# Choosing the 16 best key pairs per token from 112 rank pairs in place of 256, on VectorE alone

## The reference, cut to what matters

```python
def peer_token_block(xb, w_pq, peer_keys, peer_u, peer_v):
    qh = (xb @ w_pq).reshape(t, PEER_HEADS, 2, PEER_QDIM // 2)       # 8 heads, two halves
    s = jnp.einsum('thpc,hpkc->thpk', qh, peer_keys)                  # 128 scores for each half
    s_top, i_top = lax.top_k(s, PEER_TOPK)                            # the 16 best of each half
    cand = s_top[:, :, 0, :, None] + s_top[:, :, 1, None, :]          # 16 x 16 pairs
    cand_idx = i_top[:, :, 0, :, None] * PEER_NKEYS + i_top[:, :, 1, None, :]
    best, pos = lax.top_k(cand.reshape(t, PEER_HEADS, 256), PEER_TOPK)
    idx = jnp.take_along_axis(cand_idx.reshape(...), pos, axis=-1)    # 16 experts per head
    g = jax.nn.softmax(best, axis=-1)
    ...

def encoder_layer(...):
    ffn = channel_mixer(h, w_pq, peer_keys, peer_u, peer_v)
    ple = jax.nn.sigmoid(h @ w_pg) * (p @ w_pe)
    return layer_norm(DEEPNORM_ALPHA * h + ffn + ple, ln2_g, ln2_b)
```

## Time and profile before

| | |
|---|---|
| runs, us | 4625.53, 4610.86, 4606.46 |
| median | 4610.86 |
| span of the profiled execution | 4614.7 |
| busy, share of the span | PE 82%, DVE 73%, PEld 44%, ACT 28%, POOL 21% |
| `best_pairs` (first DMA to the last `g_low`) | about 1530.6 to 1972 us from the start |

### The profile page before, as it was taken

How to read it: one execution, slowest core, us unless ns; L and a number is a source line. 1 busy time by engine, 2 the same in 40 slices (tenths; PEclk the granted TensorE clock), 3 DMA queues, 4 the chain that set the end, 5 groups by cost and what they waited for, 6 DMA issues and landing times. The chain is left out here.

```text
span 4614.7 us, 58881 instructions
## 1 busy us (share of the span) xinstructions
PE 3770.5 (82%) x19550; PEld 2045.0 (44%) x19550; DVE 3353.4 (73%) x5560; ACT 1271.7 (28%) x2566; POOL 989.7 (21%) x1048
## 2 busy tenths in 40 slices
PE   7946667997899233389989999999999999999994
PEld 3525543553455111156644444444444445444442
DVE  1043341222589799976659999999999999999998
ACT  2132132222233111133333333333333323333321
POOL 0000000000000000000024434443444444444444
PEclk9966588998999567655579999999999999999997
DMA  2200012101110100034478898898888888888885
GB/s 87 82 3 0 0 79 101 42 14 64 43 41 26 58 0 0 0 108 134 142 252 327 327 335 316 330 341 320 322 338 330 325 334 331 332 335 330 326 321 191
DMA packets 234207, 852.35 MB, mean 185 GB/s; under 512 B 15952, under 2 KB 115088, under 8 KB 162704
## 3 DMA queue, kind: packets, MB, share of 16 engines
q0 software_dynamic: 73728, 536.90, 30.9%
q1 hardware_dynamic: 160400, 314.42, 19.6%
HBM read 790.45 MB, written 60.82 MB: 184 GB/s over the span
## 5 line engine op out<-in xcount | busy, mean ns | idle before, releaser
L69 PE MATMUL x_ps_v<-x_v_hi,x_w_hi 128*128 128x512 f16 x1536 | 605.8, 394 | 134.5 <-DVE x_w_lo L1648 73.9
L1547 POOL DMA_INDIRECT x_rows<-in_peer_uv,x_index x512 | 589.9, 1152 | 408.1 <-POOL x_index L1544 393.1
L1618 DVE SCALAR_TENSOR_TENSOR acc<-x_rows,x_share,acc 128x1024 f32<-128x1024 f32 x512 | 655.3, 1280 | 0.0
L1702 PE MATMUL x_ps_a<-h_hi,x_u_hi 128*128 128x256 f16 (+1 forms) x2048 | 620.2, 327 | 16.7 <-ACT x_u_hi L1560 16.7
L1703 PE MATMUL x_ps_a<-h_lo,x_u_hi 128*128 128x256 f16 (+1 forms) x2048 | 620.1, 327 | 0.0
L1544 POOL COPY x_index<-expert 128x1 uint32 (+1 forms) x512 | 337.8, 660 | 1260.9 <-DVE acc L1618 868.3
L70 PE MATMUL x_ps_v<-x_v_lo,x_w_hi 128*128 128x512 f16 x1536 | 603.6, 393 | 0.0
L71 PE MATMUL x_ps_v<-x_v_hi,x_w_lo 128*128 128x512 f16 x1536 | 602.2, 392 | 0.0
L1571 ACT ACTIVATE x_dots<-x_dots 128x1 f32<-128x1 f32 x512 | 103.9, 203 | 1333.7 <-DVE x_dots L1636 1333.7
L1208 POOL TENSOR_TENSOR b_hits_iota<-b_hits_iota,top_i 128x2048 f16<-128x2048 f16 x10 | 38.4, 3842 | 1917.8 <-DVE b_hits_iota L1274 1917.8
L1636 DVE CUSTOM_DVE_ANT_0 x_rows<-h_lo,x_rows 128x1024 f32<-128x1024 f32 x256 | 312.5, 1221 | 121.1 <-DMA x_rows<-in_peer_uv,x_index 120.4
(11 more groups left out here) (279 smaller groups left out, 6747.9 us busy)
## 6 DMA issues: line engine op xcount, KB each, us to landing
x_u_st<-in_peer_u_t SPq DMA_DIRECT2D x128, 512.0 KB
x_v_st<-in_peer_v SPq DMA_DIRECT2D x128, 512.0 KB
gate_scratch<-g_out SPq DMA_DIRECT2D x24, 2048.0 KB, 8.7
x_gate<-gate_scratch SPq DMA_DIRECT2D x32, 1024.0 KB
x_gate<-gate_scratch SPq DMA_DIRECT2D x32, 512.0 KB, 4.2
m_w_st<-in_w_merge SPq DMA_DIRECT2D x8, 1536.0 KB, 6.4
k_w_st<-in_w_route SPq DMA_DIRECT2D x16, 576.0 KB, 3.7
x_rows<-in_peer_uv,x_index POOLq DMA_INDIRECT x512
```

The costliest lines, as they stand in the source:

```text
L69: pe.matmul(out, lhs_hi, rhs_hi, start=first, stop=False)
L1547: pool.indirect_dma_start(rows[:, m % RING], None, uv_all, bass.IndirectOffsetOnAxis(ap=index[:, m % RING:m % RING + 1], axis=0)).then_inc ...
L1618: dve.scalar_tensor_tensor(R.acc[:, DT + tile], rows[:, r, D:2 * D], share[:, s:s + 1], R.acc[:, DT + tile], ALU.mult, ALU.add).then_inc(v ...
L1702: pe.matmul(out, u_hi[:, e, ko], R.h_hi[:, ko, t], start=ko == 0, stop=False)
```

## The change

Only `best_pairs` is changed.

- Of two descending lists of 16, only 112 rank pairs are added up as candidates: the first 4 ranks of the first half with all 16 of the second, and the other 12 ranks with the first 4 of the second. Each pair left out has at least 24 pairs that are not below it. A place among the 112 is turned into two ranks by four `scalar_tensor_tensor` steps (`place`, `rank`), where a shift and a mask did it before.
- The one-hot keeps its size, 256 x 16, but the rank is now the inner index. Each rank number is written twice side by side (`place` has a last axis of two). Both halves are multiplied by the key numbers on DVE, and the 16 products are added by halving: 8 + 8, 4 + 4, 2 + 2 and 1 + 1, each one `tensor_tensor`; the last writes both halves' key numbers to `gij`. POOL and the two reductions are gone from the stage.
- `w_st` and `cand` have their own memory. In the first tile the ten weight splits stand between the five searches, two after each. DVE waits for `steps` ahead of its first tile.
- The denominator's sum stands ahead of the addition to `R.acc` (L1304 before L1306).

The diff, cut to its core (lines of context without a sign):

```diff
+WIDE = 4
+NCAND = WIDE * TOPK + (TOPK - WIDE) * 4
+CANDS = ((0, 0, WIDE, TOPK), (WIDE * TOPK, WIDE, TOPK - WIDE, 4))
...
-        cand = sb("b_cand", [P, PH, TOPK, TOPK], f32)
+        cand = sb("b_cand", [P, PH, NCAND], f32)
...
-        place = pos[:].rearrange("p h k -> p (h k)").bitcast(f16)
...
-        pair = sb("b_hits_iota", [P, 2, TOPK, 2 * P], f16)
-        hits, iota = pair[:, 0], pair[:, 1]
+        rank = sb("b_rank", [P, 2, P], f32)
+        place = sb("b_place", [P, 2, P, 2], f16)
...
+        work = sb("b_hits", [P, KP * NT], f32)
+        hits = work[:, 0:P * TOPK].bitcast(f16).rearrange("p (n a) -> p n a", a=TOPK)
+        iota = sb("b_iota", [P, TOPK], f16)
...
-        w_st = cand[:].rearrange("p h a b -> p (h a b)").rearrange("p (s d) -> p s d", d=D)
-        p_st = pair[:].rearrange("p s a n -> p (s a n)").bitcast(f32)[:, 0:KP * NT].rearrange("p (k t) -> p k t", k=KP)
+        w_st = sb("b_w_st", [P, 2, D], f32)
+        p_st = work[:].rearrange("p (k t) -> p k t", k=KP)
...
-        LINKS = 14
+        LINKS = 19
...
-        def pick(eng, half, t):
-            names = R.top_i[:, half::2, t].rearrange("p h (a b) -> p h a b", b=1).to_broadcast([P, PH, TOPK, TOPK])
-            picked = hits[:, :, half * P:(half + 1) * P].rearrange("p a (h k) -> p h a k", h=PH)
-            return eng.tensor_tensor(picked, picked, names, ALU.mult)
-        @block.gpsimd
-        def _(pool):
-            def tile(t, s, peeled, _):
-                wait_apart(pool, hits_ok, t + 1)
-                pick(pool, 1, t).then_inc(picked_ok, 1)
-            tiles(pool, tile)
         @block.vector
         def _(dve):
-            for k in range(KW):
+            dve.wait_ge(consts, 32)
+            dve.tensor_copy(iota[:], steps[:]).then_inc(iota_ok, 1)
+            dve.wait_ge(iota_ok, 1)
+            def split_w(k):
                 dve.wait_ge(w_hi_ok, k + 1)
                 dve.scalar_tensor_tensor(w_lo[:, k], w_st[:, k % 2], WSCALE, w_hi[:, k], ALU.mult,
                                          ALU.subtract).then_inc(w_lo_ok, 1)
                 if k == 1:
                     dve.wait_ge(p_hi_ok, 1)
                     dve.tensor_tensor(p_lo[:], p_st, p_hi[:], ALU.subtract).then_inc(p_lo_ok, 1)
-            dve.wait_ge(w_lo_ok, KW)
-            dve.wait_ge(p_lo_ok, 1)
-            dve.wait_ge(consts, 32)
-            dve.tensor_copy(iota, steps[:].rearrange("p (a n) -> p a n", n=1).to_broadcast([P, TOPK, 2 * P])
-                            ).then_inc(iota_ok, 1)
-            dve.wait_ge(iota_ok, 1)
             def tile(t, s, peeled, fetched):
                 count = [0]
+                at_start = isinstance(t, int) and t == 0
                 def link(ins):
                     count[0] += 1
                     ins.then_inc(dve_in, 1)
                     wait_apart(dve, dve_in, LINKS * t + count[0])
-                if isinstance(t, int) and t == 0:
-                    pass
-                else:
+                def splits(ks):
+                    if at_start:
+                        for k in ks:
+                            split_w(k)
...
-                first = R.top_v[:, 0::2, t].rearrange("p h (a b) -> p h a b", b=1).to_broadcast([P, PH, TOPK, TOPK])
-                second = R.top_v[:, 1::2, t].rearrange("p h (a b) -> p h a b", a=1).to_broadcast([P, PH, TOPK, TOPK])
-                link(dve.tensor_tensor(cand[:], first, second, ALU.add))
-                rows = [cand[:, h].rearrange("p a b -> p (a b)") for h in range(PH)]
+                first, second = R.top_v[:, 0::2, t], R.top_v[:, 1::2, t]
+                for at, a0, n_a, n_b in CANDS:
+                    a = first[:, :, a0:a0 + n_a].rearrange("p h (a b) -> p h a b", b=1).to_broadcast([P, PH, n_a, n_b])
+                    b = second[:, :, 0:n_b].rearrange("p h (a b) -> p h a b", a=1).to_broadcast([P, PH, n_a, n_b])
+                    out = cand[:, :, at:at + n_a * n_b].rearrange("p h (a b) -> p h a b", b=n_b)
+                    last = dve.tensor_tensor(out, a, b, ALU.add)
+                link(last)
+                rows = [cand[:, h] for h in range(PH)]
                 for h in range(PH):
                     last = dve.max(best[:, h, 0:8], rows[h])
                 link(last)
+                splits((0, 1))
                 for h in range(PH):
                     last = dve.max_index(pos[:, h, 0:8], best[:, h, 0:8], rows[h])
                 link(last)
+                splits((2, 3))
                 for h in range(PH):
                     last = dve.match_replace(rows[h], best[:, h, 0:8], rows[h], LOWEST)
                 link(last)
+                splits((4, 5))
                 for h in range(PH):
                     last = dve.max(best[:, h, 8:16], rows[h])
                 link(last)
+                splits((6, 7))
                 for h in range(PH):
                     last = dve.max_index(pos[:, h, 8:16], best[:, h, 8:16], rows[h])
                 link(last)
+                splits((8, 9))
+                if at_start:
+                    dve.wait_ge(p_lo_ok, 1)
                 dve.tensor_tensor(ex[:], best[:], best[:, :, 0:1].to_broadcast([P, PH, TOPK]),
                                   ALU.subtract).then_inc(dif_ok, 1)
                 flat = pos[:].rearrange("p h k -> p (h k)")
+                twice = lambda ap: ap.rearrange("p (n a) -> p n a", a=1).to_broadcast([P, P, 2])
                 dve.tensor_scalar(part[:, 0], flat, 4, None, ALU.logical_shift_right)
-                link(dve.tensor_scalar(part[:, 1], flat, TOPK - 1, None, ALU.bitwise_and))
-                link(dve.tensor_copy(place, part[:].rearrange("p h n -> p (h n)")))
-                chosen = place.rearrange("p (a n) -> p a n", a=1).to_broadcast([P, TOPK, 2 * P])
-                dve.tensor_tensor(hits, iota, chosen, ALU.is_equal).then_inc(hits_ok, 1)
-                wait_apart(dve, hits_ok, t + 1)
-                if not (isinstance(t, int) and t == 0):
+                link(dve.tensor_scalar(part[:, 1], flat, 2, None, ALU.logical_shift_right))
+                link(dve.scalar_tensor_tensor(place[:, 0], twice(part[:, 1]), float(WIDE - WIDE * 4), twice(part[:, 0]),
+                                              ALU.add, ALU.max))
+                dve.scalar_tensor_tensor(rank[:, 0], place[:, 0, :, 0], -float(TOPK), flat, ALU.mult, ALU.add)
+                link(dve.scalar_tensor_tensor(rank[:, 1], place[:, 0, :, 0], -4.0, flat, ALU.mult, ALU.add))
+                link(dve.scalar_tensor_tensor(place[:, 1], twice(rank[:, 1]), -float(WIDE * TOPK - WIDE * 4),
+                                              twice(rank[:, 0]), ALU.add, ALU.max))
+                steps2 = iota[:].rearrange("p (m a b) -> p m a b", m=1, b=2).to_broadcast([P, 2 * P, TOPK // 2, 2])
+                chosen = place[:].rearrange("p s n (a b) -> p (s n) a b", a=1).to_broadcast([P, 2 * P, TOPK // 2, 2])
+                link(dve.tensor_tensor(hits.rearrange("p n (a b) -> p n a b", b=2), steps2, chosen, ALU.is_equal))
+                for half in range(2):
+                    names = R.top_i[:, half::2, t].rearrange("p h (k a) -> p h k a", k=1).to_broadcast([P, PH, TOPK, TOPK])
+                    picked = hits[:, half * P:(half + 1) * P].rearrange("p (h k) a -> p h k a", h=PH)
+                    last = dve.tensor_tensor(picked, picked, names, ALU.mult)
+                link(last)
+                for n in (8, 4, 2):
+                    link(dve.tensor_tensor(hits[:, :, 0:n], hits[:, :, 0:n], hits[:, :, n:2 * n], ALU.add))
+                if not at_start:
                     wait_apart(dve, t_mm, t)
-                link(pick(dve, 0, t))
-                link(dve.tensor_reduce(gij[:, 1], hits[:, :, 0:P].rearrange("p a n -> p n a"), AX.X, ALU.add))
+                link(dve.tensor_tensor(gij[:, 1:3].rearrange("p s n -> p (s n)"), hits[:, :, 0], hits[:, :, 1], ALU.add))
                 wait_apart(dve, sig, t + 1)
                 dve.scalar_tensor_tensor(s_g[:], ps_p[:], 1 / WSCALE, s_g[:], ALU.mult, ALU.mult).then_inc(prod, 1)
+                wait_apart(dve, exp_ok, t + 1)
+                link(dve.tensor_reduce(den[:, :, 0:1], ex[:], AX.X, ALU.add))
                 wait_apart(dve, prod, t + 1)
...
                 dve.tensor_tensor(R.acc[:, t], R.acc[:, t], s_g[:], ALU.add).then_inc(added, 1)
-                wait_apart(dve, exp_ok, t + 1)
-                link(dve.tensor_reduce(den[:, :, 0:1], ex[:], AX.X, ALU.add))
                 link(dve.reciprocal(den[:, :, 1:2], den[:, :, 0:1]))
-                wait_apart(dve, picked_ok, t + 1)
-                link(dve.tensor_reduce(gij[:, 2], hits[:, :, P:2 * P].rearrange("p a n -> p n a"), AX.X, ALU.add))
                 link(dve.tensor_tensor(gij[:, 0].rearrange("p (h k) -> p h k", h=PH), ex[:],
```

More of the change, by code:

```diff
@@ L1121, in best_pairs @@
         sem = lambda n: R.stack.enter_context(nc.semaphore(n))
-        NC = TOPK * TOPK
         KP = PLE // P
@@ L1149, in best_pairs @@
```

(2 more changed lines are left out.)

## The result

The changed kernel took 4494.06 us (median of 4 runs, 4484.2 to 4498.24), the kernel before on the same chip 4612.43 (4 runs): a ratio of 0.9728, interval 0.9713 to 0.9744. The forecast was 4478 with a range from 4462 to 4512. The profiled execution took 4493.93 us, 1.8 more than its span.

What follows compares the result with a forecast made beforehand. DVE was taken to set the pace of best_pairs from the first tile on. Savings of 10.9 us there and 122.1 in nine tiles took the span from 4614.7 to 4481.7; less 3.8 to the median gave 4478, range 4462 to 4512.

Steps and rivals of the forecast that it cites:

- Adding pairs and searches: Start of each tile on DVE: fewer columns save 1.13 us in the addition and 6.0 us in the searches.
- Rival 4: Searches do not get shorter, only their fixed part counting: +54, 4532 us; chance 0.03, shared with a gain partly lost elsewhere.
- Rival 1: One-hot, perhaps products and first halvings, run at 1.04 ns a column: +22 (4500) or +55 (4533 us); chance 0.11.
- Halvings: Four additions after the products on DVE: 3.56 us a tile together, the last two 0.58 each without links.
- Rival 3: Short hops in the one-hot's operations make the kernel slower, from 1.87 ns an element on: +110, 4720 us; chance 0.02.
- Links: Gaps between linked DVE steps in a tile: 0.11 us each.
- Cover: Later tiles: the sigmoid ends 4.7 us before DVE reaches its step, so neither PE nor ACT is late.
- rival 2: PE becomes the bound, staying at its lower clock for all 60 matmuls: +55, 4533 us; chance 0.07.
- First tile: Splits end at 1570.6, PE starts 4 us later, DVE waits 7.5 us, and the weights come 10.9 us earlier.
- Later stages only start earlier: Stages behind best_pairs: they only start earlier, since dense_gates reads what is complete before it begins.
- From span to median: Last step of the sum: the median of the runs lies 3.8 us below the profile's span.
- the bad end of the halvings: Halvings with every element at the reduction's price: 7.0 us without links, counted as 4.3 us worse a tile.

Runs made afterwards that it cites:

- e7: The changed kernel with PE waiting for each weight block by itself in the first tile, not for all ten: 4481.93 us, ratio 0.9698.
- e1: The kernel before with only the 112 pairs changed; its one-hot, POOL and order of splits kept: 4557.19 us, ratio 0.9857.
- e4: The changed kernel with all ten splits ahead of the first addition of pairs again: 4487.57 us, ratio 0.9709.
- e6: The changed kernel with one reduction over neighbours in place of the four halving additions: 4497.86 us, ratio 0.9730.
- e2: The kernel before with only the one-hot part changed (rank innermost, halvings, no POOL); 256 pairs and splits first kept: 4552.66 us, ratio 0.9849.
- e3: The kernel before in its old layout without POOL, both multiplications on DVE: 4608.74 us, ratio 0.9972.
- e5: The changed kernel with POOL multiplying the second half again, in the new layout: 4518.97 us, ratio 0.9770.
- e10: As e9, but DVE waits for the rank numbers only ahead of the first one-hot, and p's low part follows the eighth split: 4470.73 us, ratio 0.9666.
- e9: As e7, with g_low of a tile behind the next tile's first search: 4480.03 us, ratio 0.9688.

## Why the prediction was right, and what it missed

The direction, the engine and the mechanism were right, and the time lies 16.1 us above 4478. These 16.1 are: 1.8 from the first tile, 3.3 from the other nine, 5.7 from the stages behind, 5.8 from the step from span to median, less 0.5 elsewhere and in rounding. So the gain of the stage itself was missed by 5.1 of 133.0; the greater part lies outside the stage, where single executions differ by as much.

- **Adding pairs and searches**: forecast 1.25 and 9.70 us; 1623.70 to 1624.95 and on to 1634.64 are 1.25 and 9.69. `max_index` took 269 ns (forecast 268), `max` 260 (262). Rival 4 is excluded.
- **One-hot and products**: 2.29 and 1.22 us, as taken from L1274 and L1404. A broadcast input with inner runs of only two numbers keeps the rate. Rival 1 is excluded.
- **Halvings**: 0.62 us each for the last two, forecast 0.58. Past 0.15 fixed that is some 1.8 ns a hop, a little over the reduction's 1.67. Section 5.2 of "Vector Engine (DVE) Microarchitecture Reference" (the Trainium skill) has up to 2.5 ns for small steps, in its row for steps of 24 words; by that, as an estimate, they would have taken 0.79, and the measured 0.62 decides for these steps of 8 words. Rival 3, which needed 1.87 ns for every element, is far off: 12032 elements took 2.29 + 2.44 + 1.22 + 0.69 + 0.62 + 0.62 = 7.9 us, as priced, 0.65 ns each.
- **Links**: the term that was a little short. From the rank steps to L1302 the forecast was 10.09 us. The first tile, written out, took 10.16 (1572.63 to 1582.00, then 0.62 and the 0.17 after it). The third tile, in the loop, took 10.73: four of its gaps are 0.17, 0.19, 0.24 and 0.46, not 0.11. So the tiles after average 27.47, and those before 40.67, where the third tile, a loop tile too, gave 40.8. The nine saved 118.8, forecast 122.1.
- **Rest of a tile**: from L1302 to L1308 3.14 (forecast 3.05), and 2.47 to the next tile (2.46).
- **Cover**: DVE came 6 us behind the sigmoid in the third tile (forecast 4.7), so neither PE's row of matmuls nor the sigmoid decides. PE's mean granted clock in the tile rose from 0.67 to 0.74 and its work fell from 16.38 to 15.51 us: rival 2 had it the wrong way round.
- **First tile**: DVE had `steps` at 1539.66 (forecast 1539.5), but the splits ended at 1572.06, not 1570.6: the rounds of slot, load and ACT's high part were read from one round of the earlier trace rows, 4.8 us. Of the six rounds behind, four took 4.8 to 4.9, but two of the second slot 5.6 and 5.7 (to 1557.84 and 1564.77 above). The kernel before had shown such a round too: 5.8, from the end of its split of 1552.08 to that of 1559.09. PE to sigmoid took 18.4 (18.1). The weights came at 1594.16, not 1592.5; counted from the stage's start, 9.1 saved, forecast 10.9. That the late splits would cost PE and leave DVE idle 7.5 us was right (8.02), and e7 shows it by removing it.
- **"Later stages only start earlier"** is the step that these two profiles do not bear out, by 5.7 us. Groups of DVE in `experts`, after:

```profile
L1654 DVE CUSTOM_DVE_ANT_0 x_rows<-h_lo,x_rows 128x1024 f32<-128x1024 f32 x256 | 312.3, 1220 | 129.6 <-DMA x_rows<-in_peer_uv,x_index 129.2
...
L1654 DVE CUSTOM_DVE_ANT_0 x_rows<-h_hi,x_rows 128x1024 f32<-128x1024 f32 x256 | 311.3, 1216 | 2.7 <-DMA x_rows<-in_peer_uv,x_index 2.4 <-issue 0.2
```

The wait for gathered rows (129.2 + 2.4) is 131.6 us here and was 124.6 before. In the table, "rest" less "rows" is 2463.9 to 2467.6 us in all eleven profiles, while "rows" runs from 124.6 to 138.0 without following the edits. So the difference lies in that wait, and the code of the stage is the same. The medians speak for chance. Against the kernel before on the same chip, e1, e4, e6 and e7 took 62.6, 132.2, 122.0 and 137.9 us less, where the stage in their profiles was 62.6, 130.3, 120.8 and 136.8 shorter; so there the gain of the stage came through whole. The changed kernel itself took 118.4 less with a stage 127.9 shorter, beside a kernel before that took 4612.43 there and at least 4619.79 in the other comparisons. In e2, e3, e5 and e10 the two figures are at most 3.3 apart; e9, with 139.8 of 150.4, is the other one that falls short. Why the wait varies was not tried.
- **From span to median**: the median of before stood 3.8 below its profile's span, that of after 2.0 above. With the 1.8 around a span, the profiled execution of before would be 4616.5, 5.6 above the median of the three runs then known; that of after lies at its median (4493.93). Taking the first step over to the new kernel brought the forecast too low.
- **Slips in the working** that change nothing: the bad end of the halvings is by its own terms 3.9 us worse, not 4.3 (7.0 and four links, less 3.56), and the highest run stood 14.7 above the median, not 14.8.
